# Two weight transfers per expert in place of three in a mixture-of-experts stage

## The reference

```python
for e in range(N_EXPERTS):
    hid = jax.nn.silu(t @ w_gate[e]) * (t @ w_up[e])
    out = out + combine[:, e:e + 1] * (hid @ w_down[e]).astype(f32)
```

## Time and profile before

| what | value |
|---|---|
| time, median of 3 runs | 1832.64 us (1831.78 to 1833.19) |
| span of the profiled execution | 1829.6 us |
| median time less that span | 3.0 us |
| PE busy | 1674.6 us (92% of the span) |
| DMA, mean over the span | 216 GB/s |
| expert stage, first gate product to the end | about 1388 to 1829.6 us |

### The profile page before, as it was taken

The page is one execution under the profiler, slowest core; times in us unless marked ns, Lnnn a source line. Parts: engine busy times, 40 slices in busy tenths (PEclk is TensorE's granted clock), DMA queues, the critical chain, the costliest instruction groups (busy, mean ns, idle before and its releaser), DMA issues.

```text
span 1829.6 us, 34612 instructions
## 1 busy us (share of the span) xinstructions
PE 1674.6 (92%) x14868; PEld 1337.2 (73%) x14868; DVE 1028.7 (56%) x2171; ACT 392.6 (21%) x1001; POOL 0.2 (0%) x4
## 2 busy tenths in 40 slices
PE   7999999999999999999999999999998766757666
PEld 4565687888888886776899998788887555545554
DVE  1499979888867327887699874565423111111111
ACT  0344323221210114222222203113402100000001
POOL 0000000000000000000000000000000000000000
PEclk9999999999999999999999999999999888888988
DMA  9423324322231214654344533333479999999996
GB/s 391 182 81 116 135 113 156 138 113 114 91 141 32 118 47 158 246 171 189 139 154 169 227 120 139 139 139 116 169 320 369 426 428 428 428 429 429 428 427 290
DMA packets 36464, 395.44 MB, mean 216 GB/s; under 512 B 3968, under 2 KB 7296, under 8 KB 15232
## 3 DMA queue, kind: packets, MB, share of 16 engines
q1 hardware_dynamic: 36352, 393.84, 53.5%
HBM read 392.77 MB, written 1.05 MB: 215 GB/s over the span
## 4 chain that ended last, share of the span: by engine, by line
PE 78%; DMA 18%; DVE 2%; issue 1%; ACT 0%; SPq 0%; DVEq 0%
PE bank L2145 14%; PE bank L1855 13%; PE bank L715 13%; DMA ring<-w_moe 10%; DMA arena<-w_moe 7%; PE bank L1583 7%; PE bank L4083 3%; PE bank L2422 3%; PE bank L2468 3%; PE bank L1013 2%; PE bank L3849 2%; PE bank L2418 1%; PE bank L1318 1%; PE bank L769 1%; PE bank L4094 1%; PE bank L3075 1%
## 5 line engine op out<-in xcount | busy, mean ns | idle before, releaser
L1855 PE MATMUL bank<-arena,ring 128*128 128x256 f32 (+1 forms) x940 | 167.4, 336 | 0.0
L1855 PEld LDWEIGHTS bank<-arena,ring 128*128 128x128 f32 x940 | 148.0, 191 | 14.5 <-issue 0.4
L4235 DVE TENSOR_TENSOR arena<-arena,bank 128x128 f32<-128x128 f32 x32 | 9.2, 288 | 223.7 <-PE bank L4083 223.7
L4083 PE MATMUL bank<-arena 128*32 128x128 f32 x2008 | 78.2, 319 | 53.4 <-DMA arena<-w_moe 50.5
L2145 PE MATMUL bank<-arena 128*128 128x256 f32 x504 | 115.7, 379 | 0.0
L4083 PEld LDWEIGHTS bank<-arena 128*32 128x32 f32 x2008 | 67.4, 129 | 65.1 <-DMA arena<-w_moe 60.5
L715 PE MATMUL bank<-layer_input,ring 128*128 128x256 f32 x496 | 111.5, 381 | 0.0
L2145 PEld LDWEIGHTS bank<-arena 128*128 128x128 f32 x504 | 95.7, 190 | 13.2 <-DVE arena L2286 0.2
L715 PEld LDWEIGHTS bank<-layer_input,ring 128*128 128x128 f32 x496 | 92.8, 190 | 15.0 <-issue 2.8
L4083 PE MATMUL bank<-ring,arena 128*32 128x128 f32 x1920 | 67.9, 302 | 32.6 <-DMA ring<-w_moe 32.6
L4083 PEld LDWEIGHTS bank<-ring,arena 128*32 128x32 f32 x1920 | 58.4, 122 | 43.1 <-DMA ring<-w_moe 37.1
(11 more groups left out here) (571 smaller groups left out, 3099.1 us busy)
## 6 DMA issues: line engine op xcount, KB each, us to landing
arena<-w_moe SPq DMA_DIRECT2D x45, 2048.0 KB, 25.8
ring<-w_moe SPq DMA_DIRECT2D x45, 2048.0 KB, 26.5
ring<-w_ffn_in SPq DMA_DIRECT2D x13, 2048.0 KB, 8.1
ring<-w_ffn_in SPq DMA_DIRECT2D x7, 3072.0 KB, 10.0
ring<-w_proj SPq DMA_DIRECT2D x7, 3072.0 KB, 10.4
ring<-w_ffn_out SPq DMA_DIRECT2D x6, 2816.0 KB, 9.9
ring<-w_na_pair SPq DMA_DIRECT2D x5, 2048.0 KB, 8.2
arena<-w_far SPq DMA_DIRECT2D x16, 512.0 KB, 5.5
```

Of the source, the lines that this page charges most:

```text
L1855: last = eng.matmul(out, w[:, k * P:(k + 1) * P], x[:, k, :], start=(start and k == 0), stop=(stop and k == half - 1), skip_group_check=True)
L4083: ins = eng.matmul(bank[x][group[q], 0:P], xe[:, k, SLOTS * e:SLOTS * e + SLOTS], weight(e, first, last, (x * KT + k) * FE + q * P, P), st ...
```

## The change

For experts 4 to 30 the gate and the up part are fetched by one transfer of 4 MiB, with rows of 32 KB in place of two of 16 KB. It is issued when the up product of the slot's former expert is done, and it signals the semaphore that the gate part had. The down part keeps its own transfer. Experts 0, 1, 2, 3 and 31 are loaded as before. PE waits on that one semaphore ahead of the gate product. Its wait ahead of the up product stays in the first quad and for expert 31 (where the count is written as a constant of the same value as before), and goes in all others.

```diff
+    def load_gate_up(self, sp, x, e):
+        sp.dma_start(self.expert_slots()[e][:, 0:UPS], self.W["moe"][x][:, 0:UPS])\
+            .then_inc(self.expert_loaded()[e][0], 16)
+
...
-        for x in (RESIDENT + 1, RESIDENT + 2):
-            for part, used in enumerate(parts_used):
-                sp.wait_ge(used, x - RESIDENT)
-                self.load_part(sp, x, x - RESIDENT - 1, part)
+        for part, used in enumerate(parts_used):
+            sp.wait_ge(used, 1)
+            self.load_part(sp, RESIDENT + 1, 0, part)
+        sp.wait_ge(parts_used[1], 2)
+        self.load_gate_up(sp, RESIDENT + 2, 1)
+        sp.wait_ge(parts_used[2], 2)
+        self.load_part(sp, RESIDENT + 2, 1, 2)
         with sp.Fori(0, (LAST - RESIDENT - 3) // 2) as it:
             for e in range(2):
-                for part, used in enumerate(parts_used):
-                    sp.wait_ge(used, it * 2 + e + RESIDENT + 2)
-                    self.load_part(sp, it * 2 + e + RESIDENT + 3, e, part)
+                sp.wait_ge(parts_used[1], it * 2 + e + RESIDENT + 2)
+                self.load_gate_up(sp, it * 2 + e + RESIDENT + 3, e)
+                sp.wait_ge(parts_used[2], it * 2 + e + RESIDENT + 2)
+                self.load_part(sp, it * 2 + e + RESIDENT + 3, e, 2)
...
-                    eng.wait_ge(up_in, arrived)
+                    if first:
+                        eng.wait_ge(up_in, arrived)
+                    elif last and e == QUAD - 1:
+                        eng.wait_ge(up_in, 48)
```

## The result

The changed kernel takes 1835.71 us (median of 11 runs, 1833.76 to 1838.8) against 1832.64 before (also the median of 11). The ratio is 1.002 (95% interval 1.0013 to 1.0028), that is 2.4 to 5.1 us slower. The forecast was 1835.5.

A forecast was written before the change was run, and what follows sets the result against it. An unbroken weight stream sets when PE may start expert 30's gate product, with some 31 us of work behind it. Moved wait +4.89 and shorter stream -2.0 gave +2.9 on 1832.64: 1835.5 us, range 1833.4 to 1838.6.

The forecast's parts named there:

- The last wait moves, +4.89: At expert 30's gate product, PE must wait one transfer longer, until up 30 lands: +4.89 us.
- Earlier experts, 0: Experts 4 to 29: the same wait moves, but PE has room and the weight stream doesn't stop: cost 0.
- Rival E: Expert weight stream runs dry: engines empty for 1 us per expert, +27, 1862 us; chance 0.04.
- The stream gets shorter, -2.0: Weight stream: 27 merges save 75 ns each through fewer packets and marks, -2.0 us (1.7 to 2.3; 0 at worst).
- B: Weight stream: packets don't merge, so only the wait moves: +4.9 us, 1837.5; chance 0.12.
- D: Weight stream: each transfer carries a fixed cost, so 27 merges return 20 us: 1817 us, faster; chance 0.05.
- The clock, 0: Expert 30 after PE's idle time: gate product at half clock, scatter at full clock, as before: 0.
- C: After expert 30's gate product the cold clock runs on; with half the scatter cold, +4.7 us, 1837.3; chance 0.12.
- the sum: Whole kernel: +4.89 for the moved wait less 2.0 for the shorter stream, +2.9 us.
- F: Kernel's tail has slack, so only the shorter stream counts: -2.0 us, 1830.6; chance 0.05.
- the two terms: Expert stage: expert 30's wait moves by one transfer, +4.89 us; 27 merges shorten the stream, -2.0 us.
- The 3.0 us between median and span: Whole kernel: the median stands 3.0 us above the profiled span of 1829.6; the difference was added to the median, 1832.64.

The follow-up runs named there:

- the run that undoes it: The changed kernel, but expert 30 fetched in two transfers again with its own wait ahead of the up product: 1829.11 us, ratio 0.9983 to the kernel before.
- second profile: Each kernel run once more without edit, for its profile: 1833.81 us for the changed kernel, 1829.63 us for the kernel before.
- whole-expert run: The changed kernel with gate, up and down of experts 4 to 30 in one transfer of 6 MiB: 1858.75 us, ratio 1.0142 to the kernel before.
- run with rows of 16 KB: The changed kernel, merged transfers read from a spaced weight copy so each row goes as two 16 KB packets: 1837.93 us, ratio 1.0029 to the kernel before.

## Why the prediction was right

*The last wait moves, +4.89.* Right, by the run that merges expert 30 alone (4.85 in its trace; +5.7 by the medians, interval 3.3 to 7.5) and by the run that undoes it. Expert 30's gate product began at 1801.32 in the second profile, where the text had 1801.2. PE was idle for 5.7 to 5.8 us there, near the 6.6 of the text; no later part took over as the limit.

*Earlier experts, 0.* Right: 100.4% busy over 350 us. That share alone isn't a sharp test (97.9% went with 20 us lost in the whole-expert run), but the chain's even steps are: 58.42 and 58.40 us for four experts each. How near the edge it was can be seen from the whole-expert run: a place freed 12.4 us after a landing, with one transfer (14.5 us) behind it, let the stream run dry. The 9.2 us with four parts (19.6 us) behind didn't. Rival E had the right mechanism for that dose, and no place in this one.

*The stream gets shorter, -2.0.* Right in size: 78 ns per merge in the chain against 75, so -2.1 for 27. That 8.6 ns of it belong to the mark isn't borne out; by the run with rows of 16 KB the packets alone account for it. B (two packets per row) is what that run put back: two experts take 29.365 us again, and the time is 1.6 to 2.2 us up. D (a fixed cost per transfer) falls with the same run, for it had as few transfers as the changed kernel and gained nothing on the kernel before.

*The clock, 0.* Here a single row misled me a little. Granted clock of the changed kernel (windows, columns as in the earlier trace rows):

```profile
1804.00:1805.00 1.00, 1.00 (x24) 0.94 (x20) 0.00 (x0) 0.00 (x0) 0.00 (x0) 0.50 0.83 350
1806.00:1807.00 1.00, 1.00 (x25) 0.77 (x18) 0.00 (x0) 0.01 (x1) 0.00 (x0) 0.75 1.10 463
1807.00:1808.00 1.00, 1.00 (x5) 0.90 (x6) 0.00 (x0) 0.27 (x1) 0.00 (x0) 1.00 0.92 383
```

Cold gate product and full-clock scatter (3.72), as assumed, so C fell. But "as before" isn't one thing: that product took 3.53 us in one profile of the kernel before and 1.96 in the other, 3.37 and 3.62 in the two of the changed one. Where the kernel before happens to run it at full clock, the change costs up to 1.6 us more than the sum. How often that is, the profiles here don't settle.

F (slack in the tail) falls with the run that merges only expert 30: by the medians its whole delay reached the end (5.7 us).

*What the sum had at nothing.* Two differences lie outside the two terms and pull against each other. From expert 30's gate product to its up product the kernel before took 7.11 and 5.53 us in its two profiles, the changed kernel 6.95 and 7.20, on average 0.8 more (the clock). From that up product to the end of the span (1829.6 and 1827.9 us before, 1833.7 and 1831.7 changed) the kernel before took 24.12 and 24.14 us, the changed kernel 23.21 and 23.18, so 0.9 less; the cause of that is open. That the difference of the medians, 1835.71 - 1832.64 = 3.07 us, came within 0.2 of the forecast is therefore in part luck; the two terms are shown by themselves. The 3.0 us between median and span did no harm, since it stands on both sides of the sum. But it isn't all time outside the span: in the executions listed with both, that is 1.5 to 2.1 us, so the first profile of before was of an execution faster than the median.

## What to carry to other kernels

In a full queue the number of transfers cost nothing here, only the number of packets did. At the end of the queue a merge delays the first use by the part that is merged in. Merge in the stream, and leave the last consumer its small pieces: that version, 1829.11 us, beats both kernels. Before merging, set the stream left behind a landing against the time that the consumer needs to free the place, and leave room for the issue itself: 19.6 us against 9.2 held; 14.5 against 12.4 didn't, where the issue took 4.8 us more. Nothing between was run.

## What the runs showed of the hardware that was not expected

A packet cost 8.6 to 10 ns beside its bytes, in three comparisons (16 KB against 32 KB twice, 4 KB against 16 KB), and this was worth 18 us of 1833 when packets shrank to 4 KB. A completion mark fewer bought nothing that showed. The stage begins at 1383.4 to 1383.8 us in some executions and 1385.4 to 1386.4 in others, in the changed kernel at both; what makes the difference was not looked into.
